# Fourteen gathered u rows move from the MID stage into the DOWN stage, and MID's whole units are split

## The reference

```python
# h: 256 tokens x 2048; 8 heads, 16 picks each out of 128 x 128 experts
q = h @ w_q
v1, i1 = top_k(q[..., :half] @ k1.T, 16)         # per token and head
v2, i2 = top_k(q[..., half:] @ k2.T, 16)
top, pos = top_k(v1[:, None] + v2[None, :], 16)  # 16 experts of 16384
g = softmax(top)
act = gelu(u_tab[idx] @ h) * g
ff = sum_k act * v_tab[idx]
```

## Time and profile before

| | |
|---|---|
| median of 3 runs | 1786.73 us |
| the profiled execution, its time | 1784.72 us |
| its span, from the first to the last instruction | 1782.9 us |
| TensorE busy in the span | 1747.5 us (98%) |
| VectorE | 1520.2 us (85%) |
| ScalarE | 786.1 us (44%) |
| GpSimd | 576.3 us (32%) |
| DMA, mean | 346 GB/s |

### The profile page before, as it was taken

The page is one execution under the profiler, slowest core; times in us unless marked ns, Lnnn a source line. Parts: engine busy times, 40 slices in busy tenths (PEclk is TensorE's granted clock), DMA queues, the critical chain, the costliest instruction groups (busy, mean ns, idle before and its releaser), DMA issues.

```text
span 1782.9 us, 27711 instructions
## 1 busy us (share of the span) xinstructions
PE 1747.5 (98%) x9488; PEld 1525.2 (86%) x9488; DVE 1520.2 (85%) x2473; ACT 786.1 (44%) x1155; POOL 576.3 (32%) x388
## 2 busy tenths in 40 slices
PE   7999999999999999999999999999999999999998
PEld 5888888544999999989999999988888888888886
DVE  4668899967678999889999999979888888888887
ACT  3001222401545666434455555554555555554544
POOL 1000000011000288688878788712111111111110
PEclk9999999999999999999999999999999999999999
DMA  9999986699786677989999999999999999999994
GB/s 381 420 421 422 422 303 259 246 420 398 280 340 251 201 210 214 302 282 325 328 398 403 400 399 403 400 366 389 375 368 363 378 358 373 365 373 367 370 375 200
DMA packets 123722, 617.20 MB, mean 346 GB/s; under 512 B 42850, under 2 KB 43394, under 8 KB 52098
## 3 DMA queue, kind: packets, MB, share of 16 engines
q1 hardware_dynamic: 64258, 426.81, 61.8%
q0 software_dynamic: 53056, 184.69, 29.0%
q10 hardware_dynamic: 6338, 4.80, 0.8%
HBM read 599.22 MB, written 16.88 MB: 346 GB/s over the span
## 4 chain that ended last, share of the span: by engine, by line
PE 80%; DVE 7%; DMA 6%; issue 4%; POOL 1%; ACT 1%; DVEq 0%; SPq 0%; ACTq 0%
PE ps L1394 32%; PE ps L1049 13%; PE ps L1056 8%; PE ps L1084 6%; PE ps L1100 5%; PE ps L1042 4%; PE ps L1270 4%; PE ps L1111 2%; PE ps L1216 2%; DMA raw<-in_w_ada 2%; DMA early<-in_w_front 1%; POOL weights L537 1%; DVE w_low L1435 1%; DVE raw L1493 1%; DMA big<-in_w_gate_f 1%
## 5 line engine op out<-in xcount | busy, mean ns | idle before, releaser
L744 ACT ACTIVATE w_hi<-raw 128x1024 fp32r<-128x1024 f32 x508 | 538.1, 1060 | 489.6 <-PE ps L1394 238.4
L1435 DVE TENSOR_TENSOR w_low<-raw,w_hi 128x1024 fp32r<-128x1024 f32 x508 | 618.1, 1222 | 108.5 <-ACT w_hi L744 101.0
L537 POOL DMA_INDIRECT weights<-sel x192 | 367.7, 1915 | 236.6 <-DVE sel L1869 178.4
L1394 PE MATMUL ps<-w_hi,a 128*128 128x512 f32 x1536 | 390.3, 389 | 3.3 <-ACT w_hi L744 1.7
L1049 PE MATMUL ps<-a,w_hi 128*128 128x384 f32 x1792 | 360.0, 342 | 0.8 <-issue 0.8
L1394 PEld LDWEIGHTS ps<-w_hi,a 128*128 128x128 f32 x1536 | 288.0, 188 | 64.3 <-ACT w_hi L744 2.8
L1049 PEld LDWEIGHTS ps<-a,w_hi 128*128 128x128 f32 x1792 | 305.9, 189 | 1.7 <-issue 1.6
L1394 PE MATMUL ps<-w_low,a 128*128 128x512 f32 x1024 | 274.1, 389 | 0.0
L1056 PEld LDWEIGHTS ps<-a,w_low 128*128 128x128 f32 x1792 | 230.5, 191 | 11.5 <-DVE w_low L1435 11.0
L1056 PE MATMUL ps<-a,w_low 128*128 128x192 f32 x1792 | 233.9, 273 | 6.4 <-DVE w_low L1435 6.0
L1394 PEld LDWEIGHTS ps<-w_low,a 128*128 128x128 f32 x1024 | 191.9, 188 | 40.6 <-DVE w_low L1435 0.7
(11 more groups left out here) (230 smaller groups left out, 1789.7 us busy)
## 6 DMA issues: line engine op xcount, KB each, us to landing
raw<-in_peer_u SPq DMA_DIRECT2D x128, 1024.0 KB
raw<-in_peer_v SPq DMA_DIRECT2D x128, 1024.0 KB
early<-in_w_front SPq DMA_DIRECT2D x56, 1024.0 KB, 11.2
raw<-in_w_ada POOLq DMA_DIRECT2D x48, 1024.0 KB, 9.3
raw<-in_w_ada SPq DMA_DIRECT2D x32, 1024.0 KB, 12.6
raw<-in_peer_wq SPq DMA_DIRECT2D x16, 1024.0 KB
big<-in_w_gate_f SPq DMA_DIRECT2D x16, 1024.0 KB, 7.2
weights<-third SPq DMA_DIRECT2D x16, 768.0 KB, 18.8
```

The source lines that it names most:

```text
L537: gp.indirect_dma_start(weight_elements, bass.IndirectOffsetOnAxis(ap=put_at[:, c:c + 1], axis=0), put_gate[:, c:c + 1], None, compute_op= ...
L744: act.activation(w_hi[:, h % 2, :], raw[:, s % RING, :], ACT.Copy).then_inc(hi_ready, 1)
L1394: done = pe.matmul(ps[:, 4 * tt + 2 * (j % 2) + n, :], a, w[:, n * 512:(n + 1) * 512], start=i is None and blk == 0 and m in (0, 2), stop= ...
L1435: dve.tensor_tensor(w_low[:, s % RING, :], raw[:, s % RING, :], w_hi[:, h % 2, :].bitcast(F32), ALU.subtract).then_inc(lo_ready, 1)
```

## The change

- MID has no whole unit any more; every unit of UP and MID is split.
- MID computes 2 u rows instead of 16, both in its first iteration (units 9, 11, 13, 15). THIRD and LAST keep 24 each. The 14 rows left over (`LATE_STEPS`) are computed in DOWN's iterations 1 to 14, one in each, behind unit 9, as one reduce of 128x2048 (`late_dot`); ScalarE applies GELU to the single column behind its unit 14, and VectorE multiplies it by its gate behind unit 15 (`late_act`). They use one buffer, `got[1]`.
- The three gather buffers for u rows are used in turn from the start. The puts are placed anew: 24 behind the third row and 40 behind the fifth, then 9 per five rows.
- DOWN uses three buffers for high parts instead of two (`HIGH_AT`, `HIGH_BACK`).
- v rows have two buffers in DOWN's iterations 0 to 2 (a gather waits for the row two before it) and four from iteration 3 on; the two new ones lie where `routed` has been used up, and their first gathers wait for `at_lo`. The first iteration adds its v rows from unit 2 on instead of 6. `acc` and the copy of x for the end lie elsewhere.

```diff
-PH_MID = Phase(PH_UP, EXPERT_BLOCKS // 32, 16, plain=(1, 3, 5, 7, 9, 11, 13, 15), groups=(30, 31, 4, 11, 12, 13, 14, 15))
+PH_MID = Phase(PH_UP, EXPERT_BLOCKS // 32, 16, groups=(30, 31, 4, 11, 12, 13, 14, 15))
-FOUR_ROWS, SIX_ROWS = (1, 2, 5, 6, 9, 10, 13, 14), (0, 1, 3, 4, 5, 6, 8, 9, 11, 12, 13, 14)
-DOTS = {PH_MID: (tuple(range(8, 16)), FOUR_ROWS), PH_THIRD: (SIX_ROWS, SIX_ROWS), PH_LAST: (SIX_ROWS, SIX_ROWS)}
+TWO_ROWS, SIX_ROWS = (9, 11, 13, 15), (0, 1, 3, 4, 5, 6, 8, 9, 11, 12, 13, 14)
+DOTS = {PH_MID: (TWO_ROWS, ()), PH_THIRD: (SIX_ROWS, SIX_ROWS), PH_LAST: (SIX_ROWS, SIX_ROWS)}
+LATE_STEPS, LATE_AT = PH_DOWN.n - 2, 9
-PUTS_BEHIND = [0] + [4, 4, 3] * 5 + [2, 2, 2, 2, 1] * 10
+PUTS_BEHIND = [0, 0, 24, 0, 40] + [2, 2, 2, 2, 1] * 9
+V_PER, FOUR_FROM = ROWS // PH_DOWN.n, 3
+HIGH_AT = (0, 1, 2) * 5 + (1,)
+HIGH_BACK = [j - max(k for k in range(-PH_DOWN.per, j) if HIGH_AT[k % PH_DOWN.per] == HIGH_AT[j]) for j in range(PH_DOWN.per)]
+def v_place(step, m):
+    return m if step >= FOUR_FROM else m % 2
-SUMS_FIRST, SUMS_AT = (6, 8, 9, 10, 12, 13, 14, 15), (0, 2, 4, 6, 8, 10, 12, 14)
+SUMS_FIRST, SUMS_AT = (2, 4, 6, 8, 10, 12, 14, 15), (0, 2, 4, 6, 8, 10, 12, 14)
...
-        acc = region(28672, D)
+        x_back = region(14336, 2, D)
-        got = [region(24576 + n * D, D) for n in range(2)] + [early[:, 3072 + n * D:3072 + (n + 1) * D] for n in range(2)]
+        got = [region(24576 + n * D, D) for n in range(2)]
+        v_got = [got[0], early[:, 3072:3072 + D], region(0, D), region(D, D)]
+        acc = early[:, 3072 + D:3072 + 2 * D]
+        highs = [w_hi[:, 0, :], w_hi[:, 1, :], a2[:, 3072 + 2 * D:3072 + 2 * D + UNIT]]
...
-                    sp.wait_ge(row_used, ROWS)
+                    sp.wait_ge(row_used, EARLY_ROWS)
...
+            def late_row(n):
+                gp.wait_ge(row_used, n)
+                gather(n, u_rows, got[1], late_row_in)
+            def v_row(step, m):
+                n, place = V_PER * step + m, v_place(step, m)
+                if n == 0:
+                    gp.wait_ge(row_used, max(r for r in range(EARLY_ROWS) if ROW_BUF[r] == 0) + 1)
+                elif n == 1:
+                    gp.wait_ge(split_used, PH_DOWN.s)
+                    gp.wait_ge(at_made, 1)
+                elif step == FOUR_FROM and place >= 2:
+                    gp.wait_ge(at_lo, 3 * (place - 1))
+                else:
+                    gp.wait_ge(v_row_used, n - (3 if step > FOUR_FROM else 1))
+                gather(n, v_rows, v_got[place], v_row_in[place])
+            for step in range(PH_DOWN.n):
+                for m in range(V_PER):
+                    if 1 <= step <= LATE_STEPS and m == (2 if step > FOUR_FROM else 0):
+                        late_row(EARLY_ROWS + step - 1)
+                    v_row(step, m)
...
+                    if j == 14 and i is not None and not last:
+                        act.wait_ge(row_used, at(i, 1, EARLY_ROWS))
+                        act.activation(dots[:, late(i)], dots_now[:, 0, 0:1], ACT.Gelu).then_inc(row_gelu, 1)
...
+                    if j == 1 and i is not None:
+                        dve.wait_ge(row_acted, at(i, 1, 0))
+                    if j == LATE_AT and i is not None and not last:
+                        late_dot(i)
+                    if j == 15 and i is not None and not last:
+                        late_act(i)
...
+            def late_dot(i):
+                dve.wait_ge(late_row_in, at(i, 16, 0))
+                dve.tensor_tensor_reduce(got[1], got[1], h_tok, 1.0, 0.0, ALU.mult, ALU.add, dots_now[:, 0, 0:1])\
+                    .then_inc(row_used, 1)
+            def late_act(i):
+                dve.wait_ge(row_gelu, at(i, 1, 1))
+                dve.tensor_tensor(row_act[:, late(i)], dots[:, late(i)], row_gate[:, late(i)], ALU.mult)\
+                    .then_inc(row_acted, 1)
```

More of the change, by code:

```diff
@@ L108 @@
     first += len(peeled) // 2 + (ph.n - 1) * len(looped) // 2
[L109 to L114, removed]
+    steps += (len(peeled) > 0) + (ph.n - 1) * (len(looped) > 0)
+N_DOT_STEPS, EARLY_ROWS = steps, first
+assert EARLY_ROWS + LATE_STEPS == ROWS
+ROW_BUF = [n % 3 for n in range(EARLY_ROWS)]
+ROW_NTH = [ROW_BUF[:n + 1].count(ROW_BUF[n]) for n in range(EARLY_ROWS)]
 PUTS_SECOND, PUTS_FIRST = PEER_HEADS * TOPK // 2, PEER_HEADS * TOPK
@@ L119 @@
 PUTS_UP = 52
-PUTS_BEHIND = [0] + [4, 4, 3] * 5 + [2, 2, 2, 2, 1] * 10
-PUTS_AT = [min(PUTS_UP + sum(PUTS_BEHIND[:n]), PUTS) for n in range(ROWS + 1)]
-assert PUTS_AT[ROWS] == PUTS
-SUMS_FIRST, SUMS_AT = (6, 8, 9, 10, 12, 13, 14, 15), (0, 2, 4, 6, 8, 10, 12, 14)
+PUTS_BEHIND = [0, 0, 24, 0, 40] + [2, 2, 2, 2, 1] * 9
+PUTS_AT = [min(PUTS_UP + sum(PUTS_BEHIND[:n]), PUTS) for n in range(EARLY_ROWS + 1)]
+assert PUTS_AT[EARLY_ROWS] == PUTS
+V_PER, FOUR_FROM = ROWS // PH_DOWN.n, 3
[4 more added lines that the diff above has]
+SUMS_FIRST, SUMS_AT = (2, 4, 6, 8, 10, 12, 14, 15), (0, 2, 4, 6, 8, 10, 12, 14)
 F32 = mybir.dt.float32
@@ L363, in w_arrived, with high_at, high_back, late @@
             return w_in[n % SLOTS], 16 * (n // SLOTS + 1)
+        def high_at(ph, j):
+            return highs[HIGH_AT[j]] if ph is PH_DOWN else highs[ph.nth(j) % 2]
+        def high_back(ph, j, i):
+            return HIGH_BACK[j] if ph is PH_DOWN and (i is not None or j >= 2) else 2
+        def late(i):
+            return bass.ds(at(i, 1, EARLY_ROWS - 1), 1)
         @block.sync
@@ L542, in _ @@
             gp.wait_ge(gate_f_saved, 16)
-            for n in range(ROWS):
+            for n in range(EARLY_ROWS):
                 if ROW_NTH[n] > 1:
@@ L1921, in low_group, with down @@
                                   a_down[:, b:b + 4, 2 * P:P + TD].bitcast(F32), ALU.subtract).then_inc(at_lo, 1)
-            def down(i, last=False):
+            def down(i, four=False, last=False):
                 for j in range(PH_DOWN.per):
@@ L1937, in add_row @@
[L1937 to L1941 removed]
+                        add_row(sums_at.index(j), i, four)
+            def late_dot(i):
+                dve.wait_ge(late_row_in, at(i, 16, 0))
+                dve.tensor_tensor_reduce(got[1], got[1], h_tok, 1.0, 0.0, ALU.mult, ALU.add, dots_now[:, 0, 0:1])\
+                    .then_inc(row_used, 1)
@@ new lines, in late_act, with add_row @@
+            def late_act(i):
+                dve.wait_ge(row_gelu, at(i, 1, 1))
+                dve.tensor_tensor(row_act[:, late(i)], dots[:, late(i)], row_gate[:, late(i)], ALU.mult)\
+                    .then_inc(row_acted, 1)
+            def add_row(m, i, four):
+                n, half, cols = m // 2, m % 2, slice((m % 2) * UNIT, (m % 2 + 1) * UNIT)
+                place = v_place(FOUR_FROM if four else 0, n)
+                if half == 0 and not four:
+                    dve.wait_ge(v_row_in[place], at(i, 32, 16 * (n // 2 + 1)))
+                elif half == 0:
+                    dve.wait_ge(v_row_in[place], at(i, 16, 16 * (FOUR_FROM + 1 if place < 2 else 1 - FOUR_FROM)))
@@ L1961, in _ @@
             dve.wait_ge(row_info_in, 16 * SLICES * PEER_HEADS)
-            link(dve.tensor_tensor(row_act[:, :], dots[:, :], row_gate, ALU.mult))
+            early = slice(0, EARLY_ROWS)
+            dve.tensor_tensor(row_act[:, early], dots[:, early], row_gate[:, early], ALU.mult).then_inc(row_acted, 1)
+            dve.wait_ge(row_acted, 1)
             dve.wait_ge(gemm_evac, B_END)
             down(None)
-            with dve.Fori(1, PH_DOWN.n - 1) as i:
+            with dve.Fori(1, FOUR_FROM) as i:
                 down(i)
-            down(PH_DOWN.n - 1, last=True)
+            with dve.Fori(FOUR_FROM, PH_DOWN.n - 1) as i:
+                down(i, four=True)
+            down(PH_DOWN.n - 1, four=True, last=True)
             dve.wait_ge(gate_f_back, 16)
```

39 lines of the change are left out of this document (16 added, 23 removed).

## The result

The changed kernel takes 1795.43 us (median of seven runs, 1791.59 to 1798.51), the kernel before in the same session 1785.11 (seven, 1783.52 to 1789.48). The ratio is 1.0057, 95% interval 1.0042 to 1.0071: it is slower, by about 10 us. I had predicted 1780.9 in a range of 1773 to 1793, and 0.16 for slower.

The account below looks back on a forecast made before the run. TensorE was taken to bound THIRD, LAST and DOWN, and nearly VectorE UP. Terms -5.2 - 2.1 + 0 + 0 + 1.5 = -5.8 us on 1784.72 gave 1778.9; with the median 2.0 higher, 1780.9 us, range 1773 to 1793.

Parts of the forecast that it names:

- the DMA in DOWN: DOWN's iterations: one more u row raises the demand from 369 to 397.5 GB/s; taken as 0 us.
- The reduce on VectorE at nothing: DOWN's late rows: a 2.29 us reduce and a product fit VectorE's 4.34 us of waits an iteration; cost 0.
- The third rival: DOWN becomes bound by the DMA at 375 GB/s, 38.45 us an iteration, 1811 us in all; chance 0.08.
- The fourth rival: DOWN's third buffer gives no lead, so the late reduce costs 0.4 us or more 14 times: 1787; chance 0.10.
- The v rows in two buffers: DOWN's iterations 0 to 3: some gathers land late for VectorE; +1.5 us, bounds 0 and +16.
- the lead of 4 us: In DOWN, running some 4 us ahead was to hide most of VectorE's 1 to 3 us wait for v rows.
- the bound of 14.7: DOWN's row gathers: landing time at most 14.7 us, where four stand together.
- MID: MID's four iterations: 162.8 us instead of 168.03, -5.2 us, nearly all from late gathers gone in the second iteration.
- the one low part: UP's low part ready 0.76 us before TensorE wants it, read as VectorE's spare time in MID's first iteration.
- The way into DOWN: DOWN's start: two v rows requested later let the first blocks land sooner; -2.1 us, bounds -2.1 and 0.
- a lump: DOWN's late reduce as one VectorE instruction: 2.2 us would just miss 2.0 to spare; the third buffer was to cover it.
- The figure of 358 GB/s: The skill's HBM limit per core, by which DOWN would already be DMA-bound; set aside because THIRD ran at 400.

Follow-up runs that it names:

- e1_no_late_gather: The changed kernel without the 14 late u row gathers in DOWN, VectorE's reduces kept: 1778.64 us, 0.9963 of the kernel before.
- e2_short_dot: The changed kernel with the late reduce cut from 2048 to 128 columns, all gathers kept: 1786.28 us, 1.0010 of the kernel before.
- e11_neither: The changed kernel without the 14 late gathers and with the late reduce cut to 128 columns: 0.9975 of the kernel before.
- e9_even: The changed kernel with the five gathers of an iteration requested evenly from DOWN's iteration 4 on: 1.0044 of the kernel before.
- e5_two_highs: The changed kernel with two buffers for high parts in DOWN instead of three: 1792.17 us, 1.0046 of the kernel before.
- e6_rows_earlier: The kernel before, with MID's first-iteration u rows at the loop's units and the first two gathers 8 puts earlier: 1778.75 us, 0.9967 of the kernel before.
- e7_rows_and_start: As e6_rows_earlier, with v rows 2 to 4 of DOWN also requested later: 1775.84 us, 0.9951 of the kernel before.
- e3_spread: The changed kernel with the late reduce behind unit 11 and the late gather some 4.5 us from its neighbours: 1.0044 of the kernel before.
- e12_group_source: The changed kernel with the weights groups loaded from rows 8 KiB apart instead of 96 KiB, same bytes: 1.0046 of the kernel before.
- e8_two_halves: As e3_spread, with the late reduce as two halves behind units 9 and 11 and a small sum: 1796.70 us, 1.0058 of the kernel before.
- e4_no_groups: The changed kernel without the two 384 KiB weights group loads in DOWN's iterations 1 to 15: 1784.42 us, 0.9996 of the kernel before.

## Why the prediction was wrong

**The step that failed** is the one on the DMA in DOWN: "THIRD ran at 400 with TensorE never idle, so I take 0". Adding 1.05 MB an iteration to a stage at 369 GB/s cost 16.8 us (changed kernel against e1_no_late_gather), and 6.3 us where VectorE had no reduce to do beside it (e2_short_dot against e11_neither). The arithmetic of the demand was right, 397.5 GB/s wanted. What was wrong was to take another stage's rate as proof of room in this one. The windows of THIRD told that 400 GB/s could be moved; they did not tell how late a block lands there, nor how much of DOWN's ring was left. Blocks in DOWN went from 6.7 us (9.5 at the longest) to 8.0 (14.9, in iteration 3; 11.9 in iterations 4 to 14), of 13.6 to spare. THIRD's blocks take 8.1 at the median too, but never over 10.0. What one late block does is seen in iteration 6 of the kernel after, ScalarE's and VectorE's timelines:

```profile
1412.13 1.06 ACT L786 ACTIVATE w_hi<-raw 128x1024 fp32r<-128x1024 f32 x1 [4.62 <-DMA raw<-in_peer_v]
...
1416.66 0.85 ACT L1001 ACTIVATE a<-big 128x768 fp32r x1 [2.52 <-DVE big L1956]
```

```profile
1418.49 1.23 DVE L1480 TENSOR_TENSOR w_low<-raw,w_hi 128x1024 fp32r<-128x1024 f32 x1 [0.84 <-ACT w_hi L786]
```

ScalarE stands 4.62 us at the third block, and VectorE 2.46 us for that high part. VectorE's product of the group stands behind its low part and a v row, so ScalarE waits for it, and VectorE then idles 0.84 us more for the next high part: 3.3 us, where an iteration leaves it 1.8. TensorE then waits 0.48 us for a low part at 1423.04.

**The reduce on VectorE at nothing** was right alone (e1_no_late_gather) and wrong in its company. "The third buffer lets ScalarE be one unit further ahead" holds only while blocks are there. When a block is late, VectorE has to catch up, and by the prediction's own sum it has 1.8 us an iteration to do so in with the reduce, 4.3 without it. So the reduce costs 8.4 us beside the gathers (changed kernel against e2_short_dot). The sum had 0 for each of the two, and together they cost 14.7 us (changed kernel against e11_neither). I had costed each edit against the profile before, one by one, with the same slack as cover for both.

**The third rival** (DOWN bound by the DMA) was the right direction with the wrong form: it forecast 38.45 us an iteration at a ceiling of 375 GB/s. Iterations 4 to 14 took 37.31, the window moved 385 GB/s, iteration 3 moved 405, and the profiled e9_even moved 394 with iterations of 36.54. It was no ceiling of the rate but lateness. The fourth rival's condition, that the third buffer gives no lead, came true beside late blocks (e5_two_highs), and not for the reason it named.

**The v rows in two buffers**: +1.5 predicted. e11_neither shows 4.2 us, in iterations 1 and 3, the two places named, and e1_no_late_gather 1.8. VectorE's timeline and TensorE's, of the kernel after, at the start of iteration 1:

```profile
1216.55 1.28 DVE L2012 SCALAR_TENSOR_TENSOR early<-big,row_act,early 128x1024 f32<-128x1024 f32 x1 [2.92 <-DMA big<-in_v_rows,row_info]
```

```profile
1219.02 1.20 PE L1439 MATMUL ps<-w_low,a 128*128 128x512 f32 x4 [1.62 <-DVE w_low L1480]
```

The wait of 2.92 us lies in the 1 to 3 expected, but the lead of 4 us that was to hide most of it hid less: ScalarE had waited 2.31 us for a block just before. Gathers there landed in 10.3 us at the median and 16.4 at the longest in DOWN, against 8.1 and 11.1; the bound of 14.7 was passed.

**MID**: -5.2 predicted, -7.6 measured. The last two iterations came out as UP's (39.5 us for 39.65). Mis-sized was the first iteration: 4.2 us of waits expected, 1.3 there and 0.8 in the second. VectorE had more time in the half with the rows than the one low part that I read the earlier trace rows showed; the rest of it was not traced. The reason given for the gain, late rows of the second iteration, was right and e6_rows_earlier shows it.

**The way into DOWN**: -2.1 predicted. The first iteration went from 39.04 to 36.37 us, -2.7; e7_rows_and_start shows that the gathers are the cause, with 36.60.

**The sum** of the two profiled executions: -0.2 us ahead of MID, -7.6 in it, +0.4 from THIRD's start to DOWN's, -2.7 in DOWN's first iteration and +18.1 + 2.7 = +20.8 in the rest of DOWN, +10.7 in all, as the spans have it (1793.6 for 1782.9).

**The figure of 358 GB/s.** The Trainium skill (DMA: Bandwidth & Descriptors, Specifications) gives it as a core's limit. It was no ceiling in these runs of a single core: 405 GB/s in iteration 3 of the kernel after, 414 in DOWN's first iteration of e7_rows_and_start. The 425 for a core alone, which the prediction names beside it, stands on that page under Bandwidth, in the table of measured sizes. By 358 the kernel before, at 369, would have been bound already, so that figure gave no better warning than the row that I set against it.

**What stays open.** Why DOWN loses from 386 GB/s on while THIRD runs at 387 to 400 without a wait. The runs exclude, as most of it, the place of the gathers among each other (e3_spread, e9_even), and they exclude the pitch of the groups' rows (e12_group_source) and the reduce as a lump (e8_two_halves). Two differences were not tried alone. THIRD has six gathers and no other load beside its blocks, and DOWN has three kinds; e4_no_groups has two kinds, and its blocks of iterations 1 to 14 never take over 10.3 us, but it also moves fewer bytes. And in THIRD ScalarE waits for VectorE 7.5 us in all, in DOWN 89.8 us for its products alone (both in the kernel after). Open too is why blocks land later even without added bytes: e1_no_late_gather moves as much as the kernel before, and its blocks take 7.5 us (12.1 at the longest) against 6.7 (9.5), its row gathers 9.6 against 8.1. At that lateness next to nothing is lost (2.9 us in DOWN against 3.2).

## What to carry to other kernels

That a rate was reached in one stage doesn't show room for it in another. Before bytes are moved into a stage, read how long its prefetched blocks take from request to landing and set the longest of them, not the median, against the ring's depth. Slack must be charged once: the reduce fitted into VectorE's idle time and cost nothing alone, but the late blocks drew on the same idle time, and beside them it cost 8 us. And before work is moved away from a slow stage, look for the one iteration that is slow: here two rows requested too late and the clock behind them were all that MID had to give, and a change of three lines got it without moving a row into another stage.

## What the runs showed of the hardware

At some 370 GB/s, in DOWN's iterations 1 to 14 of the kernel before, a block of 1 MiB landed in 6.7 us and never later than 9.5; in the kernel after it was 8.0 and 14.9, the longest around iteration 3 with its 405 GB/s. In iterations 4 to 14, at 385 GB/s, the median is 7.9 and the longest 11.9, against 6.6 and 8.9 before. The added bytes are not all of the difference: with none added (e1_no_late_gather, 368 GB/s in them) these iterations have 7.5 and 10.3. After 2.92 us without matmuls TensorE's granted clock was at 1.2 GHz for the next 6 us or so the earlier trace rows; waits of TensorE of 0.96 to 1.62 us in the kernel after and of 1.94 us in e2_short_dot left it at 1.00.
